# A hybrid encoder layer on eight cores: first two tiles as a pair, earlier first norms, gate rows summed on VectorE, two buffers of normalized chunks, 4 KB weight rows

## The chip, the cores and the metric

The kernel runs on all 8 cores of one Trainium2 chip. The cores share nothing; each works on 6144 of the 49152 positions. Times are device microseconds (us) of the slowest core. The chip's engines appear as PE (TensorE, matmul; PEld its weight loads), DVE (VectorE), ACT (ScalarE), POOL (GpSimd) and SP (SyncE, which here only issues DMAs). Each engine takes its instructions in the order in which the program gives them; a semaphore wait in front of an instruction holds everything behind it on that engine.

## The reference

One layer over 16 prompt sequences of 2048 positions and 4 sample sequences of 4096, each position 1024 wide:

```python
mod = jax.nn.silu(c) @ w_ada + b_ada                    # per sequence, 3 x 1024
shift, scale, gate = jnp.split(mod, 3, axis=-1)
h = rmsnorm(x, norm_g) * (1.0 + scale) + shift
z = h @ w_in                                            # 1024 -> 4608
a, ga, u, v, gb, ma, mb = jnp.split(z, IN_SPLITS, axis=-1)
y_a = fourier_branch(a, w_fmix, b_fmix) * jax.nn.silu(ga)      # 2-D DFT over positions and group channels
y_b = sgu_branch(u, v, ...) * jax.nn.silu(gb)                  # layernorm of v, mixing inside 128 positions
merged = sigmoid(ma) * (y_a @ w_pa) + sigmoid(mb) * (y_b @ w_pb)
out = rmsnorm(x + gate * (merged @ w_out), final_g)
```

The Fourier branch needs all positions of a sequence, so `a` must be known for a whole sequence before any position can be finished. Everything else works on rows of positions.

## The kernel before

A core holds three **units** of 2048 positions, which are three prompt sequences, or one prompt sequence and one sample sequence of two units. The work goes by **tiles** of 512 positions, each of four **chunks** of 128; twelve tiles T, unit u = T // 4. The order of instructions is the order in which the Python code calls helpers. `Sched` keeps one list for each engine and puts semaphore waits before an instruction from what its operands' last writers and readers were; nothing is reordered.

**Front.** Eight 1 MB pieces of `w_ada` come on ACT's queue (`wada_off`), 32 float32 matmuls (L381) give shift and scale for three sequences, 16 small transposes (L389) turn them, and two DVE instructions make the tables `modT` and `Gtab`.

**A block** (`ABlock`): for a whole sequence only the section A of the input projection. A chunk x is loaded on SP's queue into a ring of buffers `XS`, squared and summed on ACT (`x_sq`, L442), 1/root is taken, and the chunk is scaled on DVE (`scale`, L448) to bfloat16 in `xsr`. Four chunks are a group, which `fe2` transposes on PE (32 transposes, L466) and evicts with `Gtab` and `modT`, half on DVE (L474), half on ACT (L479). `a_proj` then has for each chunk eight matmuls (L498), a cast to SBUF on DVE (L312), one first-stage matmul of the DFT (L508), an eviction on ACT or DVE and a store to `Gd` in HBM. In `body`, one pass (a **body**) goes over one group: transposes of the next group, and for each of four chunks the square of a chunk of the group after that, the projection, the first-stage matmul of the chunk before, and one scaling. The root is ACT's `Sqrt` and DVE's reciprocal here (`mode="sqrt"`), and an add and a power on POOL (`rstd`, L433 and L435) elsewhere. Block A does unit 0 (4 groups), block A2 does units 1 and 2 together (8 groups) after tile 3.

**Weights.** `w_in` lies in nine sections of 1 MB in bfloat16 (2 MB float32 in HBM, cast by POOL's DMA): A, V, GB, GA, U, MA0, MB0, MA1, MB1. Each row of a partition is 16 KB in HBM. Section 0 is asked for when piece 6 of `w_ada` is in; sections 1, 2, 3 from the `hooks1` after bodies 0, 1, 2 when a certain projection is done (`("aq", 1, m)`); sections 4 to 8, `w_pa` and `w_pb` from the hook after body 3.

**A tile** goes `v_section`, `silu_section` for GB and GA, U with a product on DVE, `sgu` (PE L686, DVE L692, POOL L697), `fourier_out` (L709 to L712), then eight times `merge_gates` and `merge` (PE L737, L743; DVE L740, L746; POOL L748), then `out_chunk` for four chunks (L610, 16 matmuls each, DVE adds x at L615), of which two are put into the next tile's sections, and `finish` (L624, store to `yu`). The Fourier data are read back from `Gd` (`g2_load`) and combined (`s3s`, L568; `s3j`, L543) between the sections of tiles 0 and 4: in tile 0 one after V, one after GB, two after GA. The normalized chunks of the next tile are made during the merges.

**Gate.** `gate_rows` (L820) multiplies the third part of `w_ada` (eight 512 KB loads) with the three conditions, 16 float32 matmuls of three columns in tile 0, and stores three rows to `gate_d`. In the first tile of each unit (`t == 0`), `w_out` is loaded anew and multiplied by the gate row on POOL (`gate_mul`, L647, eight of 128x1024), two of them in each of the last four merge steps; `out_chunk` reads the whole of `w_out`.

## Time and profile before

| | before |
|---|---|
| median of 3 runs | 1417.32 us (1414.07 to 1423.83) |
| profiled execution | 1415.01 us |
| its span, slowest core | 1413.5 us |
| spans of the cores | 1406.5 to 1413.5 us |
| granted clock of PE, mean | 0.953 to 0.959 |
| PE busy | 1245.9 us (88%) |
| DVE, ACT, POOL busy | 585.4, 503.5, 321.7 us (41, 36, 23%) |
| DMA | 149.84 MB, mean 106 GB/s |

The span runs from a core's first to its last instruction; the time of an execution is 1.5 us longer. All cores have the same program with other data, and their spans lie within 7 us, so that one core stands for all. Busy time of PE is not PE at its peak: a matmul of 512 columns takes 0.216 us from start to start at the full clock, 2.4 GHz, and 0.43 at the lower one, 1.2 GHz.

### The profile page before, as it was taken

What the parts mean: (1) busy time and instruction counts of PE and PEld (TensorE: products, weight loads), DVE (VectorE), ACT (ScalarE), POOL (GpSimd) and SP (SyncE); (2) the same over time, 40 slices, a digit from 0 to 9 for tenths busy, and PEclk for the clock granted to TensorE, in tenths of its full rate; (3) what the DMA queues carried; (4) which work ended last, traced back from release to release, by engine and by line L of the source; (5) the groups of instructions that cost most, each with busy time, mean ns of one, the idle gap of its engine ahead of it and who ended that gap; (6) DMA issues with size and microseconds to landing.
All of it is one profiled execution on the core that took longest, in us unless ns stands there. A gap on an engine that the chain in (4) does not pass through costs nothing.

```text
span 1413.5 us, 19855 instructions; the slowest of 8 cores (1406.5 to 1413.5 us)
## 1 busy us (share of the span) xinstructions
PE 1245.9 (88%) x6412; PEld 601.3 (43%) x6524; DVE 585.4 (41%) x956; ACT 503.5 (36%) x875; POOL 321.7 (23%) x398
## 2 busy tenths in 40 slices
PE   6476299699999997777996999999999699999997
PEld 1243144344444444443543444444444344444443
DVE  0353123344344445665433433444334334444344
ACT  0562213143332436664431334323343233333321
POOL 0000014413032130000145131321313613223122
PEclk9698699899999999999998999999999899999999
DMA  9899952122121255653521221212215112212111
GB/s 285 227 198 170 216 129 90 45 90 90 45 76 60 90 177 172 200 164 109 159 66 45 90 90 45 76 60 90 90 61 135 60 46 75 89 61 91 45 75 60
DMA packets 48503, 149.84 MB, mean 106 GB/s; under 512 B 5772, under 2 KB 18444, under 8 KB 45074
## 3 DMA queue, kind: packets, MB, share of 16 engines
q1 hardware_dynamic: 44514, 122.20, 25.4%
q0 software_dynamic: 2592, 17.96, 7.9%
q10 hardware_dynamic: 1296, 8.40, 1.9%
q8 instruction: 55, 0.90, 0.3%
q14 instruction: 46, 0.38, 0.1%
HBM read 135.03 MB, written 31.47 MB: 118 GB/s over the span
## 4 chain that ended last, share of the span: by engine, by line
PE 76%; DMA 8%; DVE 4%; issue 4%; ACT 4%; POOL 2%; SPq 1%; ACTq 0%; DVEq 0%; POOLq 0%
PE ps L652 41%; PE ps L610 12%; PE ps L743 6%; PE ps L737 6%; DMA Gd<-arena 5%; PE ps L662 5%; PE ps L498 2%; DMA arena<-w_ada 2%; ACT arena L442 2%; POOL arena L647 2%; PE ps L466 2%; ACT arena L479 1%; PE ps L820 1%; DMA arena<-Gd 1%; DVE arena L448 1%
## 5 line engine op out<-in xcount | busy, mean ns | idle before, releaser
L652 PE MATMUL ps<-arena 128*128 128x512 bf16 x2634 | 596.2, 380 | 7.1 <-DVE arena L692 3.7
L652 PEld LDWEIGHTS ps<-arena 128*128 128x128 bf16 x2688 | 262.4, 98 | 319.7 <-issue 8.0
L610 PE MATMUL ps<-arena 128*128 128x512 bf16 x734 | 173.9, 389 | 42.8 <-POOL arena L647 32.0
L729 ACT ACTIVATE arena<-ps 128x512 bf16<-128x512 f32 x192 | 113.2, 597 | 263.2 <-PE ps L652 259.7
L748 POOL TENSOR_TENSOR arena<-arena 128x512 bf16<-128x512 bf16 x96 | 125.1, 1303 | 283.3 <-DVE arena L746 283.3
L740 DVE TENSOR_TENSOR arena<-ps,arena 128x512 bf16<-128x512 f32 x96 | 66.4, 692 | 254.5 <-PE ps L737 254.5
L615 DVE TENSOR_TENSOR arena<-ps,arena 128x512 f32<-128x512 f32 x96 | 66.0, 691 | 189.7 <-PE ps L610 189.7
L610 PEld LDWEIGHTS ps<-arena 128*128 128x128 bf16 x768 | 75.9, 100 | 133.9 <-issue 50.1
L618 ACT ACTIVATE arena<-arena 128x1024 bf16<-128x1024 f32 x48 | 50.7, 1057 | 179.0 <-DVE arena L615 179.0
L442 ACT ACTIVATE arena<-arena 128x1024 bf16<-128x1024 f32 x96 | 100.5, 1047 | 6.1 <-DMA arena<-xB 5.9
L737 PE MATMUL ps<-arena 128*128 128x512 bf16 x384 | 98.6, 379 | 0.0
L743 PE MATMUL ps<-arena 128*128 128x512 bf16 x384 | 98.5, 379 | 0.0
L312 DVE CAST arena<-ps 128x512 bf16<-128x512 f32 (+1 forms) x114 | 64.6, 606 | 81.8 <-DMA Gd<-arena 29.3
L433 POOL TENSOR_TENSOR stat<-stat,eps_sb 128x1 f32<-128x1 f32 x92 | 17.5, 190 | 353.7 <-ACT arena L618 331.2
L498 PE MATMUL ps<-arena 128*128 128x512 bf16 x373 | 90.8, 388 | 5.1 <-DVE arena L312 3.9
L466 PE MATMUL ps<-arena 128*128 128x128 bf16 x768 | 57.9, 245 | 41.8 <-DVE arena L448 41.7
L479 ACT ACTIVATE arena<-ps,modT,Gtab 128x512 bf16<-128x512 bf16 x96 | 67.6, 775 | 75.8 <-PE ps L466 75.8
L662 PE MATMUL ps<-arena 128*128 128x512 bf16 x372 | 85.3, 383 | 0.6
L448 DVE TENSOR_SCALAR arena<-arena,stat 128x1024 bf16<-128x1024 f32 x96 | 73.4, 777 | 6.3 <-ACT arena L729 5.1
L466 PEld LDWEIGHTS ps<-arena 128*128 128x128 bf16 x768 | 54.8, 112 | 48.5 <-issue 45.5
L697 POOL TENSOR_TENSOR arena<-arena 128x512 bf16<-128x512 bf16 x48 | 53.9, 1152 | 92.9 <-DVE arena L692 92.9
L746 DVE TENSOR_TENSOR arena<-ps,arena 128x512 bf16<-128x512 f32 x96 | 66.4, 692 | 16.5 <-PE ps L743 10.3
(79 smaller groups left out, 948.7 us busy)
## 6 DMA issues: line engine op xcount, KB each, us to landing
arena<-xB SPq DMA_DIRECT2D x96, 512.0 KB, 4.0
arena<-xA SPq DMA_DIRECT2D x48, 512.0 KB, 5.1
yu<-arena SPq DMA_DIRECT2D x48, 512.0 KB, 2.8
arena<-w_in POOLq DMA_DIRECT2D x9, 1024.0 KB, 19.4
arena<-w_ada ACTq DMA_DIRECT2D x8, 1024.0 KB, 19.7
Gd<-arena SPq DMA_DIRECT2D x48, 128.0 KB, 2.6
arena<-Gd SPq DMA_DIRECT2D x12, 512.0 KB, 6.9
arena<-w_out POOLq DMA_DIRECT2D x6, 1024.0 KB, 12.8
```

Source lines behind the costliest of these rows:

```text
L442: S.op("act", lambda e: e.activation(out=xsr[:, j, :], in_=fv(XS[k], 1024), func=AF.Square, scale=0.03125, accum_out=stat[:, si, 0:1]), re ...
L448: S.op("dve", lambda e: e.tensor_scalar(out=xsr[:, j, :], in0=fv(XS[k], 1024), scalar1=stat[:, si, 1:2], scalar2=None, op0=ALU.mult), read ...
L466: fns.append(lambda e, b=b, kp=kp, kk=kk, j=j: e.transpose(psb(b)[:, kk * 512 + j * 128: kk * 512 + (j + 1) * 128], xsr[:, j, (2 * kp + kk ...
L479: S.op("act", lambda e, b=b, kk=kk, kc=kc: e.activation(out=hT[:, kc, :], in_=psb(b)[:, kk * 512:(kk + 1) * 512], func=AF.Identity, scale= ...
L498: S.pe([lambda e, kc=kc: e.matmul(ps[b][:], lhsT=hT[:, kc, j * 128:(j + 1) * 128], rhs=w_in_sb[:, 0, kc, :], start=(kc == 0), stop=(kc == ...
L610: S.pe([lambda e, b=b, dmc=dmc, half=half: e.matmul(ps[b][:], lhsT=mg[:, dmc, j * 128:(j + 1) * 128], rhs=w_out_sb[:, dmc, half * 512:(hal ...
L652: S.pe([lambda e, kc=kc: e.matmul(ps[b][:], lhsT=w_in_sb[:, sec, kc, col:col + 128], rhs=hT0[:, kc, :], start=(kc == 0), stop=(kc == 7)) f ...
L662: S.pe([lambda e, kc=kc, b=b, j=j: e.matmul(ps[b][:], lhsT=hT0[:, kc, j * 128:(j + 1) * 128], rhs=w_in_sb[:, SEC["V"], kc, :], start=(kc = ...
L729: S.op("act", lambda e, b=b, so=so: e.activation(out=bv(so, 512), in_=ps[b][:], func=AF.Sigmoid), reads=[("ps", b)], writes=gk(so, 1024))
L737: S.pe([lambda e, k=k: e.matmul(ps[b][:], lhsT=w_pa_sb[:, k, dmc * 128:(dmc + 1) * 128], rhs=sga[:, k, :], start=(k == 0), stop=(k == 3)) ...
L743: S.pe([lambda e, k=k: e.matmul(ps[b2][:], lhsT=w_pb_sb[:, k, dmc * 128:(dmc + 1) * 128], rhs=sgb[:, k, :], start=(k == 0), stop=(k == 3)) ...
L748: S.op("pool", lambda e: e.tensor_tensor(out=mg[:, dmc, :], in0=mg[:, dmc, :], in1=bv(sl[1], 512), op=ALU.add), reads=mk + gk(sl[1], 1024) ...
```

## The change

- **First norms under the load.** The squares and scalings of groups 0 and 1 stand ahead of the adaLN matmuls; chunks 0 to 3 are loaded at once, 4 to 7 when piece 7 of `w_ada` is in. `fe2` is split in `fe_t` (transposes) and `fe_e` (evictions); group 0's transposes stand ahead of the adaLN evictions.
- **Two buffers of normalized chunks.** Groups alternate between `O_XSR` and a second place. Squares are written to a scrap buffer. `sq` now does a pair of chunks: two squares, one `rstd` of width 2 on POOL, always by add and power, and two scalings; it stands ahead of the projections of chunks 0 and 2 of a body. The ring of A2 has 6 chunks instead of 8. Block A takes a sixth group, tile 1's.
- **Tiles 0 and 1 as a pair**, with a second set of buffers (`TB1`, in the place of Z of the other units): V for both, GB for both, and so on; the Fourier pieces stand after GB of tile 0, GB of tile 1, GA of tile 0, GA of tile 1. Output chunks of tile 0 stand after the pair, those of tile 1 in the sections of tile 2.
- **Gate.** Each unit's row is summed on VectorE: eight loads of 128x1024, eight multiply-adds with a condition column (`gate_acc`), then a sum over partitions by two float32 matmuls with a matrix of ones (`gate_sum`). Unit 0 in the merges of tile 0 through two buffers, unit 1 in the merges of tile 2 through one, unit 2 in the sections of tile 3 through three. `gate_mul` is spread: one in each of merge steps 1 to 6, two in step 7.
- **4 KB rows.** The weights lie in HBM as blocks of 1024 columns, so that one row of a transfer is 4 KB; `w_in`, `w_pa`, `w_pb` and `w_out` are loaded so.
- In tile 4 `w_out` is asked for after U instead of before it, and the last two Fourier pieces stand there.

```diff
+    def blocks(t, k):
+        return dram_ap(t, k * 512 * 1024, [[1024, 128], [128 * 1024, 4], [1, 1024]])
+
     def w_sec(s, after=()):
-        S.dma("pool", [lambda e: e.dma_start(
-            out=bv(O_WIN + 8192 * s, 4096), in_=w_in.ap()[s * 128:(s + 1) * 128, :])],
-            "s_w%d" % s, reads=after, writes=wink[s])
+        S.dma("pool", [lambda e: e.dma_start(out=bv(O_WIN + 8192 * s, 4096).rearrange("p (k n) -> p k n", k=4),
+                                             in_=blocks(w_in, s))], "s_w%d" % s, reads=after, writes=wink[s])
...
-    def rstd(n, src, dst, rk, wk, mode):
-
-        if mode == "sqrt":
-            S.op("act", lambda e: e.activation(out=dst, in_=src, func=AF.Sqrt, scale=1.0, bias=eps_sb[:, 0:1]),
-                 reads=rk + ["eps"], writes=wk)
-            S.op("dve", lambda e: e.reciprocal(out=dst, in_=dst), reads=wk, writes=wk)
-        else:
-            S.op("pool", lambda e: e.tensor_tensor(out=dst, in0=src, in1=eps_sb[:, 0:1].to_broadcast([128, n]), op=ALU.add),
-                 reads=rk + ["eps"], writes=wk)
-            S.op("pool", lambda e: e.tensor_tensor(out=dst, in0=dst, in1=mh_sb[:, 0:n], op=ALU.pow),
-                 reads=wk + ["mh"], writes=wk)
...
+    def rstd(n, src, dst, rk, wk):
+
+        S.op("pool", lambda e: e.tensor_tensor(out=dst, in0=src, in1=eps_sb[:, 0:1].to_broadcast([128, n]), op=ALU.add),
+             reads=rk + ["eps"], writes=wk)
+        S.op("pool", lambda e: e.tensor_tensor(out=dst, in0=dst, in1=mh_sb[:, 0:n], op=ALU.pow),
+             reads=wk + ["mh"], writes=wk)
...
+    def sq_op(k, si, junk, jk):
+        S.op("act", lambda e: e.activation(out=junk, in_=fv(XS[k], 1024), func=AF.Square, scale=0.03125,
+                                           accum_out=stat[:, 0, si:si + 1]),
+             reads=gk(XS[k], 4096), writes=jk + [("st", si)])
+
+    def scale_op(k, j, si, xoff):
+        xr = bv(xoff + 2048 * j, 1024)
+        S.op("dve", lambda e: e.tensor_scalar(out=xr, in0=fv(XS[k], 1024), scalar1=stat[:, 1, si:si + 1],
+                                            scalar2=None, op0=ALU.mult),
+             reads=gk(XS[k], 4096) + [("st1", si)], writes=gk(xoff + 2048 * j, 2048))
...
+    def gate_load(kc, k):
+        S.dma("sp", [lambda e: e.dma_start(out=fv(XS[k], 1024), in_=w_ada.ap()[kc * 128:(kc + 1) * 128, 2048:3072])],
+              "s_x%d" % k, writes=gk(XS[k], 4096))
+
+    def gate_acc(u, kc, k, acc):
+
+        c = cs_sb[:, kc * 3 + u:kc * 3 + u + 1]
+        if kc == 0:
+            S.op("dve", lambda e: e.tensor_scalar(out=fv(XS[acc], 1024), in0=fv(XS[k], 1024), scalar1=c, scalar2=None,
+                                                  op0=ALU.mult),
+                 reads=gk(XS[k], 4096) + ["cs"], writes=gk(XS[acc], 4096))
+        else:
+            S.op("dve", lambda e: e.scalar_tensor_tensor(out=fv(XS[acc], 1024), in0=fv(XS[k], 1024), scalar=c,
+                                                         in1=fv(XS[acc], 1024), op0=ALU.mult, op1=ALU.add),
+                 reads=gk(XS[k], 4096) + gk(XS[acc], 4096) + ["cs"], writes=gk(XS[acc], 4096))
...
+            S.pe([lambda e, b=b, h=h: e.matmul(ps[b][:], lhsT=ones_sb[:], rhs=fv(XS[acc], 1024)[:, h * 512:(h + 1) * 512],
+                                               start=True, stop=True)],
...
+        def sq(self, g, h):
+            self.load_to(4 * g + 2 * h + 2)
+            si = stat2(2)
+            for j in (2 * h, 2 * h + 1):
+                sq_op(self.slot(g, j), si + j % 2, bv(O_TYB, 1024), gk(O_TYB, 2048))
+            rstd(2, stat[:, 0, si:si + 2], stat[:, 1, si:si + 2], [("st", si), ("st", si + 1)],
+                 [("st1", si), ("st1", si + 1)])
+            for j in (2 * h, 2 * h + 1):
+                scale_op(self.slot(g, j), j, si + j % 2, self.xoffs[g % 2])
+                self.load_to(4 * g + j + 1 + len(self.ring))
...
         def body(self, hooks):
             for q in range(self.nq):
                 self.fe(q + 1)
                 for j in range(4):
-                    if q + 2 <= self.nq:
-                        self.sq(q + 2, j)
-                    st1 = a_proj(q, j, self.f, 4 * q + j, self.N1)
+                    if q + 2 < len(self.dst) and j % 2 == 0:
+                        self.sq(q + 2, j // 2)
+                    st1 = a_proj(self.dst[q][0], j, self.f, 4 * q + j, self.N1)
                     if self.pend:
                         self.pend.pop(0)()
                     self.pend.append(st1)
-                    self.scales(2)
-                self.scales()
                 if q in hooks:
...
-        gb = [newbank(), newbank()]
-        for kc in range(8):
-            S.pe([lambda e, kc=kc, h=h: e.matmul(ps[gb[h]][0:3, :], lhsT=cs_sb[:, kc * 3:kc * 3 + 3],
-                                                 rhs=fv(XS[kc], 1024)[:, h * 512:(h + 1) * 512],
-                                                 start=(kc == 0), stop=(kc == 7)) for h in range(2)],
...
+    A = ABlock(1, 4, list(range(8)), 16,
+               lambda i: rowsA(i) if i < 16 else rowsB((i - 16) // 4, i % 4),
+               [(hoffs[0], 0), (hoffs[1], 0), (hoffs[0], 0), (hoffs[1], 0), (O_HT, 0), (TB1.h, 0)],
+               (O_XSR, O_Z + 16896))
+    A.load_to(4)
+    S.dma("sp", tabs[1:], "s_tab", writes=["tabs"])
+    tabs = []
+    A.load_to(8, after=gk(wada_off[7], 512))
     A.group(0)
-    A.fe(0)
     A.group(1)
...
+    fe0 = fe_t(A.xoffs[0])
+    for cb in range(4):
+        evict(mrow[0:3, cb * 512:(cb + 1) * 512], ps[mb[cb]][0:3, :], [("ps", mb[cb])], gk(O_MROW + 2048 * cb, 2048))
...
+    fe_e(fe0, hoffs[0], 0)
...
+    pair = (T0, TB1)
+    s3_begin(1)
+    A.fe(5)
+    for tb in pair:
+        v_section(tb)
+    for i, tb in enumerate(pair):
+        silu_section(tb, SEC["GB"], tb.sgb, tb.b)
+        s3s(i)
+    for i, tb in enumerate(pair):
+        silu_section(tb, SEC["GA"], tb.sga, tb.a)
+        s3s(2 + i)
+    w_out_load()
+    gate_load(0, 0)
+    gate_load(1, 1)
+    for tb in pair:
+        u_section(tb)
+    for i, tb in enumerate(pair):
+        sgu(tb)
+        fourier_out(tb, 0, i)
+    merge_gates(T0, 0)
+    for dmc in range(8):
+        if dmc + 1 < 8:
+            merge_gates(T0, dmc + 1)
+        else:
+            merge_gates(TB1, 0)
+        merge(T0, dmc)
+        if dmc % 2 == 0:
+            for k in range(2):
+                gate_acc(0, dmc + k, k, 2)
+                if dmc + k + 2 < 8:
+                    gate_load(dmc + k + 2, k)
+    gate_bias(128, 3)
+    x_load(0, rowsB(2, 0))
+    x_load(1, rowsB(2, 1))
+    sc = []
+    for dmc in range(8):
+        if dmc + 1 < 8:
+            merge_gates(TB1, dmc + 1)
+        merge(TB1, dmc)
+        if dmc == 0:
+            gate_sum(128, 2, 3)
+        else:
+            for k in ((dmc - 1,) if dmc < 7 else (6, 7)):
+                gate_mul(XS[3], k)
+        if dmc in (1, 2, 4, 5):
...
-            if t == 0 and dmc >= 4:
-                gate_mul(u, 2 * (dmc - 4))
-                gate_mul(u, 2 * (dmc - 4) + 1)
+                merge_gates(tb, dmc + 1)
+            merge(tb, dmc)
+            if t == 0 and dmc:
+                for k in ((dmc - 1,) if dmc < 7 else (6, 7)):
+                    gate_mul(O_WIN, k)
+            if T == 2:
+                if dmc:
+                    gate_acc(1, dmc - 1, 6, 7)
+                gate_load(dmc, 6)
...
             A2.fe(0)
             A2.sq(1, 0)
+            out_chunk(tb, T, 0, OS[0])
             A2.sq(1, 1)
-            out_chunk(T, 0, OS[0])
-            A2.scales()
-            A2.sq(1, 2)
-            A2.sq(1, 3)
-            out_chunk(T, 1, OS[1])
-            A2.scales()
-            A2.body({0: lambda: (finish(), out_chunk(T, 2, OS[2])), 1: lambda: (finish(), out_chunk(T, 3, OS[3])),
+            out_chunk(tb, T, 1, OS[1])
```

On DVE, in one body of block A2: before, a reciprocal or one scaling (L448) at a time stands between the casts (L312, of the projections and of every other first stage), and the first two waits of a body are for ACT's root.

```order
L474 TENSOR_SCALAR arena<-ps6,Gtab,modT 128x512
L431 RECIPROCAL stat<-stat 128x1 [waits act]
L312 CAST arena<-ps0 128x512 [waits pe]
L312 CAST arena<-ps1 128x512 [waits pe,s_gw3]
L431 RECIPROCAL stat<-stat 128x1 [waits act]
L312 CAST arena<-ps2 128x512 [waits pe]
L448 TENSOR_SCALAR arena<-arena,stat 128x1024 [waits s_x8,dve]
L431 RECIPROCAL stat<-stat 128x1 [waits act]
L312 CAST arena<-ps4 128x512 [waits pe]
L312 CAST arena<-ps5 128x512 [waits pe,s_gw1]
```

The same place after: evictions are L460, scalings L427, casts L313.

```order
L460 TENSOR_SCALAR arena<-ps6,Gtab,modT 128x512
L427 TENSOR_SCALAR arena<-arena,stat 128x1024 [waits s_x4,pool]
L427 TENSOR_SCALAR arena<-arena,stat 128x1024 [waits s_x5]
L313 CAST arena<-ps0 128x512 [waits pe,dve]
L313 CAST arena<-ps1 128x512 [waits pe,dve,s_gw3]
L313 CAST arena<-ps2 128x512 [waits pe,dve]
L427 TENSOR_SCALAR arena<-arena,stat 128x1024 [waits s_x6,pool]
L427 TENSOR_SCALAR arena<-arena,stat 128x1024 [waits s_x7]
L313 CAST arena<-ps4 128x512 [waits pe,dve]
```

Two scalings with a wait for POOL now stand ahead of the cast of chunk 0, and two more ahead of that of chunk 2.

On PE, from the last transposes of the A block of unit 0 on: before (L662 is V, L652 the other sections, L568 and L576 the Fourier pieces).

```order
L662 MATMUL ps<-arena 128x512 x32
L568 MATMUL ps<-arena 128x128 x16
L576 MATMUL ps<-arena 128x64 x4
L652 MATMUL ps<-arena 128x512 x32
L568 MATMUL ps<-arena 128x128 x16
```

After (V is L687, the other sections L677, Fourier pieces L557 and L565, transposes L447):

```order
L447 MATMUL ps<-arena 128x128 x32
L687 MATMUL ps<-arena 128x512 x64
L677 MATMUL ps<-arena 128x512 x32
L557 MATMUL ps<-arena 128x128 x16
L565 MATMUL ps<-arena 128x64 x4
L677 MATMUL ps<-arena 128x512 x32
L557 MATMUL ps<-arena 128x128 x16
```

96 section matmuls stand ahead of the first Fourier piece where 32 stood, and 32 transposes of tile 1 ahead of them.

On POOL, the weight loads behind block A: before, sections 1 to 6 follow one another with nothing between.

```order
L837 DMA arena<-w_sT 128x512
L369 DMA arena<-w_in 128x4096 [waits pe]
L369 DMA arena<-w_in 128x4096 [waits pe,s_w0]
L369 DMA arena<-w_in 128x4096 [waits pe,s_wa5]
L369 DMA arena<-w_in 128x4096 [waits s_wa4]
L369 DMA arena<-w_in 128x4096 [waits s_wa7]
```

After, from section 2 on:

```order
L373 DMA arena<-w_in 128x4x1024 [waits pe,s_w0]
L408 TENSOR_TENSOR stat<-stat,eps_sb 128x2 [waits act,dve]
L410 TENSOR_TENSOR stat<-stat,mh_sb 128x2 [waits pool]
L408 TENSOR_TENSOR stat<-stat,eps_sb 128x2 [waits act,dve]
L410 TENSOR_TENSOR stat<-stat,mh_sb 128x2 [waits pool]
L373 DMA arena<-w_in 128x4x1024 [waits pe,s_wa5]
```

The same four instructions stand once more between section 3 and section 4: every section now goes out behind the norms (L408, L410) of a body, which wait for ACT's squares; before, section 4 stood right behind section 3.

## Rows read from the trace of the kernel before

**Rows 1.** The page, busy tenths of PE in 40 slices of the span.
```profile
PE   6476299699999997777996999999999699999997
```

**Rows 2.** Waits of PE, whole span: waiting line, releaser; total, times, longest, us.
```profile
PE ps L466 <- DVE arena L448: 41.7, 10, 9.8
PE ps L610 <- POOL arena L647: 32.0, 3, 10.7
PE ps L568 <- DMA arena<-Gd: 25.2, 1, 25.2
```

**Rows 3.** DMA of the first 40 us: packets, MB and rate.
```profile
DMA packets 2733, 11.71 MB, mean 293 GB/s; under 512 B 937, under 2 KB 937, under 8 KB 1693
```

**Rows 4.** Timeline of the opening, PE: start, length, engine, line, what, [idle before].
```profile
39.45 3.59 PE L381 MATMUL ps<-arena,cs_sb 128*3 128x512 f32 x8 [1.22 <-DMA arena<-w_ada]
44.08 1.12 PE L389 MATMUL ps<-id_sb,arena 3*128 3x3 f32 x16 [1.04 <-ACT arena L442]
...
65.09 3.15 PE L466 MATMUL ps<-arena 128*128 128x128 bf16 x28 [9.78 <-DVE arena L448]
```

**Rows 5.** Timeline of PE from 120 to 206 us.
```profile
132.72 8.22 PE L662 MATMUL ps<-arena 128*128 128x512 bf16 x31
166.13 1.86 PE L568 MATMUL ps<-arena 128*128 128x128 bf16 x16 [25.20 <-DMA arena<-Gd]
...
192.08 13.89 PE L820 MATMUL ps<-arena,cs_sb 128*3 128x512 f32 x32
```

**Rows 6.** Chain of waits around the Fourier data of unit 0: start, length, what.
```profile
145.93 14.53 DMA Gd<-arena
160.63 5.26 DMA arena<-Gd
```

**Rows 7.** Timeline of three bodies of the second A block.
```profile
606.54 3.33 PE L466 MATMUL ps<-arena 128*128 128x128 bf16 x32 [2.57 <-DVE arena L448]
...
611.31 1.05 ACT L442 ACTIVATE arena<-arena 128x1024 bf16<-128x1024 f32 x1
...
620.82 1.95 PE L466 MATMUL ps<-arena 128*128 128x128 bf16 x32 [2.57 <-DVE arena L448]
...
624.64 1.06 ACT L442 ACTIVATE arena<-arena 128x1024 bf16<-128x1024 f32 x1
...
626.38 1.29 DVE L312 CAST arena<-ps 128x512 bf16<-128x512 f32 x2
...
627.33 0.38 PE L508 MATMUL ps<-arena 128*128 128x512 bf16 x1 [0.89 <-ACT arena L442]
...
632.61 1.41 DVE L448 TENSOR_SCALAR arena<-arena,stat 128x1024 bf16<-128x1024 f32 x2
...
634.16 1.95 PE L466 MATMUL ps<-arena 128*128 128x128 bf16 x32 [2.57 <-DVE arena L448]
```

**Rows 8.** Timeline of GpSimd: add and power of width 1, then power of width 4.
```profile
538.96 0.19 POOL L433 TENSOR_TENSOR stat<-stat,eps_sb 128x1 f32<-128x1 f32 x1 [8.69 <-ACT arena L618]
...
539.29 0.55 POOL L435 TENSOR_TENSOR stat<-stat,mh_sb 128x1 f32<-128x1 f32 x1
...
280.82 1.02 POOL L435 TENSOR_TENSOR bnag<-bnag,mh_sb 128x4 f32<-128x4 f32 x1
```

**Rows 9.** Timeline at the end of the merges of the first gated tile.
```profile
258.00 4.22 POOL L647 TENSOR_TENSOR arena<-arena 128x1024 bf16<-128x1024 bf16 x2
...
262.86 1.49 PE L610 MATMUL ps<-arena 128*128 128x512 bf16 x3 [10.67 <-POOL arena L647]
```

**Rows 10.** Timeline of two more operations, then DMA issues: count, size, median us to landing.
```profile
208.69 4.49 POOL L697 TENSOR_TENSOR arena<-arena 128x512 bf16<-128x512 bf16 x4 [21.58 <-DVE arena L692]
...
282.06 2.48 DVE L624 SCALAR_TENSOR_TENSOR arena<-arena,stat 128x1024 f32<-128x1024 f32 x2
...
arena<-xB SPq DMA_DIRECT2D x96, 512.0 KB, 4.0
...
arena<-w_ada SPq DMA_DIRECT2D x8, 512.0 KB, 12.9
```

445 lines of the change are left out of this document (233 added, 212 removed).

## The prediction

> **What bounds the kernel now.** I read the page first: the profiled execution took 1415.0 us, its slowest core's span is 1413.5 us, so 1.5 us lie around the span, and the median of the runs is 1417.3 us. PE is busy in nine tenths of most slices; the low ones stand in the first fifth of the span and around slices 15 to 19 [rows 1]. That is where time can be won: some 1246 us of PE work stay whatever the order. Next the waits of PE over the whole span [rows 2]: transposes waiting for normalized chunks (VectorE L448) 41.7 us in 10 waits, output projections waiting for gate multiplies (GpSimd L647) 32.0 us in 3, and one 25.2 us wait for the Fourier data of unit 0. Then the timeline of the opening and the chain of waits, to see which wait ends last there.
>
> The opening goes so. The adaLN weights come in at 293 GB/s with the DMA engines full [rows 3], the last adaLN matmul starts at 39.4 us, and only then are x chunks normalized; the transposes of group 1, which I call T(1), start at 65.1 [rows 4]. Four bodies of four chunks follow; tile 0's V section starts at 132.7 at a low clock (8.2 us; at the full one 31 such matmuls take 6.9), then PE waits until 166.1 [rows 5], because the last store of the Fourier data was on its way for 14.5 us after it was issued [rows 6]: 16 KB rows of weights filled the DMA engines. At 192.1 PE spends 13.9 us on float32 gate matmuls with three columns [rows 5].
>
> **The change part by part,** as differences in us of the span.
>
> *Front end.* The bytes that must land before the second group is transposed are the same: w_ada 8.4 MB, eight chunks 4.2, section 0 2.1, 14.7 MB in all; at [rows 3]'s rate they end near 48 us. The order changes: chunks 4 to 7 are asked for only when the last adaLN piece is in. ScalarE's adaLN evictions stand behind the square of chunk 7, VectorE's behind its scaling. So: 47.5, square 1.1 [rows 7], GpSimd pair 1.2, two scalings 1.4, two row copies 1.4 (the last two took 1.04 ahead of the small transposes [rows 4]), sixteen small transposes 1.1, and T(1) starts near 54, 11 us earlier.
>
> *Bodies of the A blocks (two buffers, chunks normalized in pairs).* This is the term that decides. A body is T, four projections, four first-stage matmuls. I take the old one from [rows 7]: T at 620.8, then ScalarE's four evictions and at 624.6 the square (T + 3.8), root and reciprocal, the cast at 626.4, the first-stage matmul at 627.3 (T + 6.5); the scalings hold the next T until 634.2. T to T is 14.3 and 13.3, mean 13.8. Now VectorE's row has two scalings ahead of the cast that the first-stage matmul needs, and they wait for two squares and for GpSimd. T + 3.8 squares start; second square ends at + 6.2 (1.25 and 1.15); GpSimd add and power of width 2: 0.14, 0.33 and a power between 0.55 (width 1) and 1.02 (width 4) [rows 8], 0.7, so + 7.4; two scalings + 8.9; cast 0.7 and 0.25: first-stage matmul at T + 9.8. PE has finished T and two projections at + 5.2, so it waits 4.6 us. The same again for the second pair: 0.5 to ScalarE's eviction, 0.5 until its square starts, 2.4, 1.2, 1.5, 0.7, 0.25, that is 7.1; the matmul 0.2. Next T at T + 17.0. The wait of T for scalings goes, as meant, and a longer one takes its place in the middle of the body. At the low clock the squares start 1.0 later (611.3 is T + 4.8, against 3.8) [rows 7], so 18.0; I take 17.4, the clock being low in part. Bounds: 13.3 (the pair order costs nothing) and 18.7 (low clock in both halves).
>
> The first block: four bodies at 17.4, 2.3 for ScalarE's eight extra evictions in the first, 3.5 for the channel tables, 2 for the transposes of tile 1: V starts at 54 + 77.4 = 131.4 instead of 132.7: **-1.3**. The second block: seven bodies with squares, 3.6 each, and 2 more at its entry, where the pair stands ahead of the output additions: **+27**.
>
> *The pair.* Before the first Fourier blocks are needed there is now V, V and GB, 20.7 us, where there was V. The last store is issued near 132. The seven late weight loads now stand on GpSimd's queue behind the norms of the last body, near 129 instead of 99 to 115, so the stores meet a less filled DMA, and 4 KB rows let them between. Block 0 landed 5.3 us after its load was asked for [rows 6]; even 12 us would be in time for 153. So the 25.2 go, **-25.2**, and 1 of low clock, **-1**. The late weights (seven of 2.1 MB at [rows 3]'s rate, 50 us) are in by 180; the first used of them, U, is due at 188: hidden. It costs 15 us if they start 20 late. Two sgu stages in a row run into GpSimd's product of 1.12 us a head [rows 10] with a ring of two: PE waits for banks, **+3.6** (0 to 6). Everything else of the two tiles is the same PE work.
>
> *Gates.* Matmuls of 13.9 go, two float32 matmuls with a matrix of ones come, 0.86 each (L381's four, in eight records, took 3.6) [rows 4]: **-12.1**. Units 1 and 2 had their gates from the same pass, so they pay the two matmuls again: **+3.4**. The 24 multiply-adds of 1.24 us (two of that form took 2.48) [rows 10] lie on VectorE beside 5.2 us of PE per step, under the matmuls. In tile 2 they go through one buffer: load, add, load. With 4.0 us to land, as xB chunks do, and 1.3 for the add with its wait, a turn is 5.5 against 5.2: **+2** (bounds 0, and the rival below).
>
> *Gate multiplies spread over the merges.* At the end of a gated tile GpSimd had two merge additions and four multiplies left; now one addition and two multiplies. Four multiplies take 8.4 us (4.2 for two), of which half goes, and PE's 10.7 us wait [rows 9] becomes 6.7: three times **-4.0**, -12 (bounds -6 and -24).
>
> Sum: -1.3 + 27 - 25.2 - 1 + 3.6 - 12.1 + 3.4 + 2 - 12 = -15.6, a span of 1398. With 1.5 around it 1399.4; the median before was 2.3 above the profiled execution, and I say **1401 us**, 1.2% less. Over 1% is about what a measurement of this kernel can tell from no change.
>
> **The rivals.** *A: the pair order costs nothing in the bodies.* For it: most of the 41.7 us [rows 2] are what a second buffer is there to remove. Against: VectorE takes its instructions in order. With 13.3 per body the second block gives -3.5 instead of +27, and V starts 16 earlier in the first: 1401 - 46 = 1355, or 1372 where late weights and Fourier loads then bind the pair. *B: the clock falls in every body.* After the same 2.57 us wait T took 3.33 us once and 1.95 twice [rows 7], at 1.2 and 2.4 GHz; with waits of 4.6 and 3.3 us in each body both halves may start low: 18.7 instead of 17.4, eleven times, +14: 1415. The Trainium skill (TensorE: Matmul & The Clock Gate, HAM oscillation) describes a kernel whose every step begins at half clock because a wait stands in each; by that rule B is what happens, and the trace agrees in one body of three. *C: the gate's single buffer paces tile 2* (slower). The SyncE queue puts each gate load behind the multiply-add of the one before, and x loads and stores behind it; VectorE, waiting for a load, holds the merge products, and PE runs out of banks. It decides from 5 us landing. The gate loads of before took 12.9 us in the median [rows 10], though eight at once beside weights: 12.9 + 1.5 - 5.2 is 9.2, eight times 74, 1475; at 8 us 34, 1435. For it: nothing hides a turn. Against: the DMA engines are mostly idle there, and a lone chunk lands in 4.0. *D: the cut rows do not free the stores.* If a store still takes some 27 us and the Fourier blocks come at 178, PE waits 24 at 154 and the pair buys next to nothing: 1425. The Trainium skill (DMA: Bandwidth & Descriptors, SWDGE vs HWDGE vs iDMA) says an engine changes rings only between packets, preferably of at most 4096 bytes; by that the cut rows should shorten each turn fourfold, which speaks against D; no row here has such rows.
>
> **How the numbers follow.** Forecast (1385 to 1410) 0.42, A 0.22, B 0.15, C 0.11, D 0.10. The forecast's own range comes from its bounds: the bodies 16.7 to 17.8, the front end 5 either way, multiplies and sgu. The range for all reaches into A at its bound side and into D, 1364 to 1430; C beyond it and the fast end of A are left out, 2 in 10. Faster by over 1% (under 1403): A and three fifths of the forecast, with a little, 0.52. Within 1%: the rest of the forecast, B: 0.30. Slower: C, most of D's upper side and B's: 0.18.
>
> **What would show it.** T to T in the second block near 17, with waits of PE L497 (first stage) for VectorE of 4 to 5 us twice a body, and the waits of the transposes for the scalings gone; V of tile 0 near 131; no wait of L557 for the Fourier load above 2 us; L610 waiting for GpSimd 6 to 7 us three times; tile 2's merges at 5.2 us a step. What would make it wrong: bodies of 14 us (A), transposes of 3.4 us in all of them (B), merge steps over 6 us in tile 2 (C), PE idle at GB or U of the pair (D).

## The result: 1% slower

The changed kernel took 1433.2 us in the median of four runs (1431.2 to 1434.9), the kernel before 1420.6 beside it: ratio 1.0104, 95% interval 1.0056 to 1.0151. I had said 1401, with a range up to 1430, and a gain. The profiled execution has a span of 1432.2 us against 1413.5, so 18.7 us are to be found. By the medians they are 12.6: the traced execution of the kernel before, 1415.0 us, was 5.6 us below the median of its runs here, so that a span compared with its span looks some 6 us worse than the medians do. Ratios and medians here and below are over the runs in which no die was slowed.

The page of the changed kernel, PE and its clock in 40 slices, then two rows of DMA issues (count, size, median us to landing):

```profile
PE   6566799989989896677898999999999899999997
PEclk9798899999999998888999999999999999999999
...
arena<-w_ada SPq DMA_DIRECT2D x24, 512.0 KB, 4.8
...
Gd<-arena SPq DMA_DIRECT2D x48, 128.0 KB, 3.5
```

The low slices stand where they stood [rows 1], in the first fifth and, counted from 0, at 15 to 18. The waits of PE over the whole span show what changed (waiting line, releaser; us in total, times, longest):

```profile
PE ps L497 <- DVE arena L313: 65.9, 25, 5.1
PE ps L604 <- POOL arena L672: 18.9, 3, 6.3
PE ps L879 <- DVE arena L313: 14.1, 1, 14.1
...
PE ps L651 <- DVE arena L639: 10.1, 2, 5.2
PE ps L557 <- DMA arena<-Gd: 7.5, 2, 7.1
PE ps L447 <- DVE arena L427: 7.1, 1, 7.1
```

The 41.7 us of transposes waiting for scalings [rows 2] are 7.1 now. In their place the first stage (L497) waits 65.9 us for casts, the small transposes (L879) 14.1, and the ones matmuls (L651) 10.1, a wait that I had not named. The 32.0 us for gate multiplies are 18.9, the 25.2 for the Fourier data 7.5.

One body of the second A block, timeline of PE and of VectorE (start, length, engine, line, what, [idle before]); it answers to [rows 7]:

```profile
605.50 1.95 PE L447 MATMUL ps<-arena 128*128 128x128 bf16 x32
607.29 1.89 PE L487 MATMUL ps<-arena 128*128 128x512 bf16 x8
609.01 0.38 PE L497 MATMUL ps<-arena 128*128 128x512 bf16 x1
609.23 1.89 PE L487 MATMUL ps<-arena 128*128 128x512 bf16 x8
615.27 0.58 PE L497 MATMUL ps<-arena 128*128 128x512 bf16 x1 [4.15 <-DVE arena L313]
615.65 3.62 PE L487 MATMUL ps<-arena 128*128 128x512 bf16 x8
619.06 0.63 PE L497 MATMUL ps<-arena 128*128 128x512 bf16 x1
619.49 2.40 PE L487 MATMUL ps<-arena 128*128 128x512 bf16 x8
622.44 0.38 PE L497 MATMUL ps<-arena 128*128 128x512 bf16 x1 [0.55 <-DVE arena L313]
```

```profile
613.00 1.42 DVE L427 TENSOR_SCALAR arena<-arena,stat 128x1024 bf16<-128x1024 f32 x2 [3.77 <-POOL stat L410]
614.33 1.88 DVE L313 CAST arena<-ps 128x512 bf16<-128x512 f32 x3
620.16 1.42 DVE L427 TENSOR_SCALAR arena<-arena,stat 128x1024 bf16<-128x1024 f32 x2 [3.96 <-POOL stat L410]
```

VectorE idles 3.77 us ahead of two scalings whose rstd is not there, while casts that could run stand behind them; PE gets its first-stage input 9.8 us after T, at 615.27. Behind its wait the third projection takes 3.62 us, 1.2 GHz, and the next part of the fourth is still slow. T to T is 17.2 (605.50, 622.65), as forecast. At the end of the body PE waits only 0.55 us, where I had said 3.3: the projections at the low clock fill that time, and the period is set by ScalarE, GpSimd and VectorE.

Where the 18.7 us come from, segment by segment, against the terms of the prediction (differences of the changed kernel's span from the kernel before; the starts are those of [rows 4, 5 and 7] and of the timelines here):

| stretch | said | measured |
|---|---|---|
| T(1) of the first block | -11.1 | -2.7 (62.4) |
| from there to V of tile 0 | +9.8 | +16.5 (V at 146.5) |
| V of tile 0 to the first merges, both tiles | -36.5 | -29.1 |
| ones matmul of unit 0 | +1.7 | +2.2 |
| gate multiplies of tile 0 | -4 | -5.4 |
| tile 1's own transposes, which went ahead of V | 0 | -2.6 |
| gates of units 1 and 2, in tiles 2 and 3 | +5.4 | +20.8 |
| second A block | +27 | +25.7 |
| the rest, with two sets of gate multiplies | -8 | -6.6 |
| sum | -15.7 | +18.8 |

Up to rounding the columns add up to the prediction's -15.6 and to the 18.7. The transposes of tile 1 are a slip of my sum: their 2 us were charged to the first block and not taken off where they had stood. Each stretch is from one traced execution of either kernel. Three stretches carry the miss: the opening with the first block, the Fourier data, and above all the gates of tiles 2 and 3.

### The profile page after: what moved, and what is told of

It is laid out like the page before. It is cut to its first block, busy times and chain, and to the rows that moved or that the text cites. A ratio compares the mean times of both kernels' runs of the same rounds, so it can differ in the third digit from the quotient of the medians.

```text
span 1432.2 us, 20068 instructions; the slowest of 8 cores (1425.6 to 1432.2 us)
## 1 busy us (share of the span) xinstructions
PE 1269.4 (89%) x6504; PEld 602.3 (42%) x6504; DVE 610.8 (43%) x933; ACT 485.2 (34%) x818; POOL 352.7 (25%) x442
## 4 chain that ended last, share of the span: by engine, by line
PE 70%; DMA 11%; DVE 5%; ACT 5%; issue 5%; POOL 3%; SPq 0%; ACTq 0%; DVEq 0%; POOLq 0%
PE ps L677 38%; PE ps L604 11%; PE ps L773 5%; PE ps L767 5%; PE ps L687 4%; DMA arena<-w_ada 4%; DMA arena<-Gd 3%; ACT arena L421 3%; DMA Gd<-arena 2%; ACT arena L465 2%; DVE arena L313 1%; PE ps L487 1%; POOL stat L410 1%; DMA arena<-xA 1%; POOL arena L672 1%
## 5 line engine op out<-in xcount | busy, mean ns | idle before, releaser
L677 PE MATMUL ps<-arena 128*128 128x512 bf16 x2688 | 602.6, 380 | 1.7 <-DVE arena L724 1.6
L677 PEld LDWEIGHTS ps<-arena 128*128 128x128 bf16 x2688 | 262.7, 98 | 319.6 <-issue 8.4
L604 PE MATMUL ps<-arena 128*128 128x512 bf16 x768 | 178.8, 391 | 28.8 <-POOL arena L672 18.9
L408 POOL TENSOR_TENSOR stat<-stat,eps_sb 128x1 f32<-128x1 f32 (+1 forms) x114 | 25.3, 222 | 509.4 <-ACT arena L612 317.5
L427 DVE TENSOR_SCALAR arena<-arena,stat 128x1024 bf16<-128x1024 f32 x96 | 71.5, 771 | 166.5 <-POOL stat L410 166.4
L604 PEld LDWEIGHTS ps<-arena 128*128 128x128 bf16 x768 | 76.2, 100 | 125.0 <-issue 41.9
L612 ACT ACTIVATE arena<-arena 128x1024 bf16<-128x1024 f32 x48 | 50.7, 1057 | 186.5 <-DVE arena L609 186.5
L487 PE MATMUL ps<-arena 128*128 128x512 bf16 x384 | 112.2, 446 | 0.3 <-ACT arena L465 0.3
L773 PE MATMUL ps<-arena 128*128 128x512 bf16 x384 | 98.6, 379 | 0.0
L767 PE MATMUL ps<-arena 128*128 128x512 bf16 x384 | 98.5, 379 | 0.0
L313 DVE CAST arena<-ps 128x512 bf16<-128x512 f32 (+1 forms) x114 | 62.7, 602 | 62.3 <-PE ps L557 21.2
L687 PE MATMUL ps<-arena 128*128 128x512 bf16 x384 | 84.7, 379 | 0.0
L497 PE MATMUL ps<-arena 128*128 128x512 bf16 x48 | 22.1, 460 | 65.9 <-DVE arena L313 65.9
L776 DVE TENSOR_TENSOR arena<-ps,arena 128x512 bf16<-128x512 f32 x96 | 66.3, 691 | 16.7 <-PE ps L773 11.2
L410 POOL TENSOR_TENSOR stat<-stat,mh_sb 128x1 f32<-128x1 f32 (+1 forms) x114 | 67.7, 594 | 17.3 <-POOL stat L408 1.5
```

The costliest lines, as they stand in the source:

```text
L313: S.op("dve", lambda e: e.tensor_copy(out=dst, in_=src), reads=reads, writes=writes)
L410: S.op("pool", lambda e: e.tensor_tensor(out=dst, in0=dst, in1=mh_sb[:, 0:n], op=ALU.pow), reads=wk + ["mh"], writes=wk)
L487: S.pe([lambda e, kc=kc: e.matmul(ps[b][:], lhsT=hT[:, kc, j * 128:(j + 1) * 128], rhs=w_in_sb[:, 0, kc, :], start=(kc == 0), stop=(kc == ...
L604: S.pe([lambda e, b=b, dmc=dmc, half=half: e.matmul(ps[b][:], lhsT=tb.mg[:, dmc, j * 128:(j + 1) * 128], rhs=w_out_sb[:, dmc, half * 512:( ...
L677: S.pe([lambda e, kc=kc: e.matmul(ps[b][:], lhsT=w_in_sb[:, sec, kc, col:col + 128], rhs=tb.hT[:, kc, :], start=(kc == 0), stop=(kc == 7)) ...
L687: S.pe([lambda e, kc=kc, b=b, j=j: e.matmul(ps[b][:], lhsT=tb.hT[:, kc, j * 128:(j + 1) * 128], rhs=w_in_sb[:, SEC["V"], kc, :], start=(kc ...
```

## The experiments

Each was timed beside the kernel before; the ratio is to the runs of the same batch. The span is that of the profiled execution, and times at single stages are from that one execution.

| kernel | median us | ratio to before, 95% interval | span us |
|---|---|---|---|
| changed | 1433.2 | 1.0104 (1.0056 to 1.0151) | 1432.2 |
| e1_lag | 1387.4 | 0.9769 (0.9723 to 0.9814) | 1385.7 |
| e2_front | 1431.5 | 1.0063 (1.0037 to 1.0089) | 1429.8 |
| e3_gates | 1424.2 | 1.0014 (0.9991 to 1.0038) | 1425.3 |
| e4_rows16 | 1457.2 | 1.0243 (1.0208 to 1.0277) | 1455.5 |
| e5_pipe | 1374.9 | 0.9652 (0.9636 to 0.9669) | 1373.7 |
| e6_before_rows4 | 1410.2 | 0.9904 (0.9886 to 0.9923) | 1410.1 |
| e8_best | 1359.9 | 0.9549 (0.9534 to 0.9565) | 1356.7 |
| e9_order | 1340.4 | 0.9450 (0.9431 to 0.9469) | 1338.2 |
| e10_mul | 1337.4 | 0.9431 (0.9407 to 0.9456) | 1335.5 |
| e11_onebuf | 1357.4 | 0.9569 (0.9545 to 0.9593) | 1353.2 |
| e12_all | 1316.0 | 0.9246 (0.9222 to 0.9271) | 1312.2 |
| e13_after_order | 1430.3 | 1.0058 (1.0039 to 1.0076) | 1426.9 |

### The order on VectorE

**e1_lag.** The scalings of a pair stand behind the second cast after them.

```diff
                 for j in range(4):
                     if q + 2 < len(self.dst) and j % 2 == 0:
-                        self.sq(q + 2, j // 2)
+                        sc.append(self.sq(q + 2, j // 2, lag=True))
...
                     self.pend.append(st1)
+                    if sc and j % 2:
+                        sc.pop(0)()
```

> The changed kernel, but in both A blocks the two scalings of a pair stand on VectorE's queue behind the cast of the second projection after them, not ahead of the cast of the first. Theory (VectorE's order is the cost of the pairs: it stands 5.73 and 3.91 us a body in front of a scaling whose rstd is not there, with ready casts behind it): the waits of the first stage (L497) for the cast, 4.2 and 1.7 us, go; the last scaling of a body now ends about 11.5 us after its transposes began, so that the period of the second block falls from 17.2 to about 12, 8 times 5 = 41 us less, and about 3 times 4 less in the first block: near 1385 to 1395 us. Rival (the bodies are bound by something else that would show up at once, the six-chunk ring and its loads, or the chain square, square, rstd, scale, scale of two pairs, 3.8 + 3.8 us and the evictions ahead of them): the period stays at 16 or more and the time within 5 us of 1433.

The theory held, and the order turned out to be the whole term: with it changed the second block is faster than in the kernel before (115.1). From T(1) to the V of tile 4 the second block took 108.6 us instead of 140.7, from T(1) to the V of tile 0 the first took 74.2 instead of 84.1; the span is 46.5 less. I had said a period of 12, 41 and 12 us less; it was 32.1 and 10.0. One period, PE:

```profile
575.41 3.57 PE L447 MATMUL ps<-arena 128*128 128x128 bf16 x32 [2.03 <-DVE arena L427]
578.78 2.88 PE L487 MATMUL ps<-arena 128*128 128x512 bf16 x8
...
587.32 0.38 PE L497 MATMUL ps<-arena 128*128 128x512 bf16 x1
589.82 2.52 PE L447 MATMUL ps<-arena 128*128 128x128 bf16 x32 [2.12 <-DVE arena L427]
```

The period of 14.4 here and 13.5 behind it, where I had said 12, is the wait for the last scaling and the clock behind it: transposes of 3.57 and a projection of 2.88 where the full clock gives 1.95 and 1.89. The next kernel takes both away.

**e5_pipe.** Squares and rstd stand one pair ahead of the scalings.

```diff
                     if q + 2 < len(self.dst) and j % 2 == 0:
-                        self.sq(q + 2, j // 2)
+                        self.scales(q + 2, j // 2)
+                        g, h = (q + 2, 1) if j == 0 else (q + 3, 0)
+                        if g < len(self.dst):
+                            self.squares(g, h)
```

> The changed kernel, but the squares and rstd of a pair stand one pair ahead of its scalings, so that each scaling finds its rstd ready. In the kernel with the scalings behind the second cast the period of the second block was 13.5 us, of which 2.1 to 2.8 are a wait of the transposes for the last scaling, and another 2 are transposes and first projection at the low clock behind that wait. Theory (the order on VectorE was the whole cost of the pair; ScalarE, VectorE and TensorE each have 9 to 10 us of work a body): the period falls to 10 to 11, the second block from its second transposes to the V of tile 4 from 140.7 us to 85 to 90; the first block gains at most as much as with the lag, since stores of Gd wait there for the DMA; 1370 to 1380 us. Rival (the six-chunk ring or the eight stores and loads on SyncE's queue take over at once): the period stays at 13 or more, near 1390.

The period is 10.0:

```profile
575.87 1.95 PE L447 MATMUL ps<-arena 128*128 128x128 bf16 x32
...
585.66 0.38 PE L497 MATMUL ps<-arena 128*128 128x512 bf16 x1
585.87 1.95 PE L447 MATMUL ps<-arena 128*128 128x128 bf16 x32
```

PE goes from transposes to transposes at 2.4 GHz; the rival, a ring of six chunks or SyncE's queue, did not show. The second block took 93.9 us, 47 less than in the changed kernel; I had said 85 to 90, and the first three bodies, which also hold output projections, are the difference (T to T 17.0, 14.6 and 11.1). The first block took 69.7, 4.5 less than in e1_lag, where I had said that it gains no more than there; PE stood 17.6 us of it before one first-stage matmul, as it did in e8_best below.

**e11_onebuf.** One buffer of normalized chunks instead of two, in e8_best.

```diff
-               (O_XSR, O_Z + 16896))
+               (O_XSR, O_XSR))
...
-                        [(hoffs[g % 2], 1 + g // 4) for g in range(8)] + [(O_HT, 1)], (O_XSR, XS[10]),
+                        [(hoffs[g % 2], 1 + g // 4) for g in range(8)] + [(O_HT, 1)], (O_XSR, O_XSR),
```

> The combined version with one buffer of normalized chunks in both A blocks instead of two. Theory (the second buffer is worth little: what cost the kernel before 41.7 us of waits of transposes for scalings was that squares, rstd and scalings of a chunk stood in the same body; with the squares a pair ahead a scaling can run as soon as the transposes of that body have read the buffer): the period of the second block stays at 10 to 11 and the time within 4 us of 1361. Rival (the second buffer is what the second block lives on, and the order only lets it work): the period rises to 12 or more, 15 us or more in all.

The second block took 94.2 us against 93.8 with two buffers, the ratios agree within their intervals. Under this order the second buffer bought nothing; under the order of the changed kernel, or of the kernel before, it was not tested. Rival A of the prediction was right that a body of 13 us and less was to be had, and wrong that the buffer would give it.

### Rows of 4 KB, and what stands ahead of a store

**e4_rows16.** The changed kernel with weights in rows of 16 KB.

```diff
-        S.dma("pool", [lambda e: e.dma_start(out=bv(O_WIN + 8192 * s, 4096).rearrange("p (k n) -> p k n", k=4),
-                                             in_=blocks(w_in, s))], "s_w%d" % s, reads=after, writes=wink[s])
+        S.dma("pool", [lambda e: e.dma_start(out=bv(O_WIN + 8192 * s, 4096), in_=w_in.ap()[s * 128:(s + 1) * 128, :])],
+              "s_w%d" % s, reads=after, writes=wink[s])
```

> The changed kernel with the weights again in rows of 16 KB instead of 4 KB. Theory (rows decide how long a store of 128 KB stands behind the weights, but the first block is held by VectorE's order and by the total of bytes): stores in the first block take longer than in the changed kernel, the wait for the first Fourier load grows from 7.1 us to 10 or more, the time is 0 to 8 us more, up to 1441. Rival (4 KB rows cost more descriptors on GpSimd's queue and slow the weights down): 3 to 8 us less.

The direction was right, the size, 23.3 us of span, three times what I had allowed. In the first block the rows changed nothing, against what I had said: V starts at 145.1 against 146.5. The waits of PE, first of this kernel, then of the changed kernel's timeline at the same place, with its issue of the four Fourier loads and, from its chain of waits, the last store and the fourth of the loads:

```profile
PE ps L557 <- DMA arena<-Gd: 30.1, 1, 30.1
```

```profile
160.35 7.07 PE L677 MATMUL ps<-arena 128*128 128x512 bf16 x32
174.56 1.86 PE L557 MATMUL ps<-arena 128*128 128x128 bf16 x16 [7.13 <-DMA arena<-Gd]
...
157.39 11.03 SPq L520 DMA_DIRECT2D arena<-Gd  x4
...
146.28 10.94 DMA Gd<-arena
159.35 41.73 DMA arena<-Gd
```

With rows of 16 KB the last store takes 25.8 us instead of 10.9, the Fourier loads are asked for at 170.8 instead of 157.4, and the first block of them is used at 196.1 instead of 174.6. With all of the change but the rows the stall is longer than it was before (25.2), not shorter: with either rows the last seven weight loads are issued near 140 to 146 us, at the last stores, and in the kernel before at 99 to 115. There they were in when the first Fourier load was asked for, and it took 5.3 us [rows 6]. In the changed kernel they land until 208: the first Fourier load takes 16.7 us, the fourth 41.7, and PE waits 7.1 us for the first and reaches the others at most 2 us after they land.

**e6_before_rows4.** The same rows in the kernel before, nothing else.

```diff
-        S.dma("pool", [lambda e: e.dma_start(
-            out=bv(O_WIN + 8192 * s, 4096), in_=w_in.ap()[s * 128:(s + 1) * 128, :])],
+        S.dma("pool", [lambda e: e.dma_start(
+            out=bv(O_WIN + 8192 * s, 4096).rearrange("p (k n) -> p k n", k=4), in_=blocks(w_in, s))],
```

> The kernel before, with the weights in rows of 4 KB and nothing else. With 16 KB rows the changed kernel waited 30.1 us for its first Fourier load instead of 7.1, and took 23 us more. Theory (the rows, not the pair, took most of the 25.2 us stall away): the stall before the first Fourier blocks falls from 25.2 to 5 to 10 us and the time by 15 to 20, near 1402 to 1408. Rival (it is the pair's cover, V and V and GB instead of V alone, and rows only matter on top of it): the stall stays over 18 and the time within 7 us of the kernel before.

Neither story as I wrote it. The waits of PE for the Fourier data, total, times, longest:

```profile
PE ps L571 <- DMA arena<-Gd: 23.7, 2, 21.1
```

The rows brought the first Fourier block from 166.1 to 155.9, half of it as an earlier V (127.7 against 132.7), and 1.0% of the time by the ratio, 14 us; the spans of the two traced executions differ by 3.4 alone. But the stall stays at 21: the block comes 28.2 us after V starts, in the changed kernel 28.0, in e5_pipe 28.5. The pair covers that with its own work and leaves 7. The last stores take 8.6 to 10 us here instead of 14.5 to 27, but the load behind them takes 15.0 instead of 5.3, with the weights still under way. So the rows and the pair each did a part of what I had booked for the pair. The pair without the rows, in the kernel before, was not run; e4_rows16 suggests that it would have bought nothing at this place.

**e9_order.** e8_best (below) with V's and GB's weights after the third body, the final norm's table after the block.

```diff
-        tab(fg_bc, dram_ap(final_g, 0, [[0, 128], [1, D]]))
...
-        0: lambda: (late_tabs(), w_s_load(), w_sec(1, after=[("aq", 1, 0)])),
-        1: lambda: w_sec(2, after=[("aq", 1, 4)]),
-        2: lambda: (channel_tables(), w_sec(3, after=[("aq", 1, 8)])),
+        0: lambda: (late_tabs(), w_s_load()),
+        2: lambda: (channel_tables(), w_sec(1), w_sec(2), w_sec(3)),
```

> The combined version, with the weights of V and GB loaded after the third body of the first block instead of after the first and second, and the final norm's table after the block instead of after its first body. In the combined version TensorE stands 19.6 us in the third body, since a cast waits for the place of a store of Gd that was issued near 82 us behind 3 MB of tables and weights and landed near 105. Theory (the order of the bytes is that wait, their sum sets the first Fourier load, 34 to 35 MB by 154 us in the combined version): the wait falls under 8 us, V starts at 113 to 118 instead of 127.2, but V and GB may wait for their own weights, and the first Fourier block starts within 4 us of 153.9; time within 4 us of 1361. Rival (the stores' lateness is what delays the Fourier loads): the first Fourier block starts before 148 and 6 to 10 us go.

The reason for trying it, in e8_best: the chain of waits in the first block, and PE behind it.

```profile
79.22 27.09 DMA Gd<-arena
...
107.02 0.69 DVE arena L313
...
107.96 0.58 PE ps L497
```

One store of 128 KB took 27.1 us, and the cast that needs its place waited; the bodies, at 10 us each, had caught up with the DMA. My theory fell, the rival held: the longest wait for a cast went from 19.6 to 4.3 us, V started at 111.0 instead of 127.2, and the first Fourier block at 137.4 instead of 153.9, 16.5 earlier with the same weights to come. The span fell by 18.5 us, where the rival had said 6 to 10. PE of e9_order there:

```profile
111.00 13.98 PE L686 MATMUL ps<-arena 128*128 128x512 bf16 x64
124.81 7.07 PE L676 MATMUL ps<-arena 128*128 128x512 bf16 x32
137.35 1.86 PE L556 MATMUL ps<-arena 128*128 128x128 bf16 x16 [5.48 <-DMA arena<-Gd]
```

Nothing waited for V's or GB's weights. It was not the sum of the bytes that held this block back, but which of them stood ahead of the stores.

**e13_after_order.** The same edit in the changed kernel alone.

```diff
-        0: lambda: (late_tabs(), w_s_load(), w_sec(1, after=[("aq", 1, 0)])),
-        1: lambda: w_sec(2, after=[("aq", 1, 4)]),
-        2: lambda: (channel_tables(), w_sec(3, after=[("aq", 1, 8)])),
+        0: lambda: (late_tabs(), w_s_load()),
+        2: lambda: (channel_tables(), w_sec(1), w_sec(2), w_sec(3)),
```

> The changed kernel with only the later loads of V's and GB's weights and of the final norm's table. In the changed kernel the third body of the first block waits 4.2, 3.6 and 3.4 us for casts, two of them for the place of a store of Gd that is still under way. Theory (the order of the bytes is worth what VectorE's own order leaves of it): the bodies of the first block all take 17 to 18 us, V of tile 0 starts near 139 instead of 146.5, the first Fourier block near 167 instead of 174.6: 7 us less, near 1426. Rival (as in the combined version, the stores' lateness costs the whole block): 15 to 20 us less, near 1416.

V of tile 0 at 139.0, the first Fourier block at 166.7: these two as the theory said. The span is 5.3 less, for 7. In the changed kernel a store of 21.6 us stood in its third body (the chain of waits):

```profile
94.60 21.57 DMA Gd<-arena
```

ScalarE's eviction waited 11.1 us for its place, and the squares, the rstd, the scalings and the casts stood behind; the store before it, of 21.1 us, held a cast 5.9 us by itself. The third body took 27.4 us there and takes 19.2 here. The intervals of the ratios, 1.0058 and 1.0104, overlap, so that the gain in time is not shown by itself; the reading rests on the stages of one traced execution each.

### The opening

**e2_front.** The norms of chunks 4 to 7 behind the adaLN evictions and the first evictions of transposes.

```diff
     A.group(0)
-    A.group(1)
...
     fe_e(fe0, hoffs[0], 0)
+    A.group(1)
     A.body(hooks1)
```

> The changed kernel, but the norms of chunks 4 to 7 stand behind the adaLN evictions and behind the evictions of the first transposes. Theory (the 14.1 us for which TensorE stands before its 3x3 transposes have two covers: the order on ScalarE and VectorE, and behind it the landing of chunks 4 to 7 at 49 to 55 us, which is the DMA's doing): the 3x3 transposes start near 47 us instead of 60.7, the second transposes still wait for chunk 7 and start near 59.5 instead of 62.4, the first projection near 61.5 instead of 66.3: 5 us less in all, near 1428. Rival (the order alone is the cost): the second transposes start near 50 and 10 to 13 us go, near 1421.

The small transposes started at 46.1, but T(1) at 60.5 instead of 62.4, and the span is 2.4 us less: half of what I had said, and the chunks' landing, not the order, is what holds T(1). ScalarE of the changed kernel in the opening:

```profile
25.01 1.06 ACT L421 ACTIVATE arena<-arena 128x1024 bf16<-128x1024 f32 x1 [3.98 <-DMA arena<-xA]
...
49.98 1.06 ACT L421 ACTIVATE arena<-arena 128x1024 bf16<-128x1024 f32 x1 [23.82 <-DMA arena<-xA]
...
55.47 1.06 ACT L421 ACTIVATE arena<-arena 128x1024 bf16<-128x1024 f32 x1 [0.61 <-DMA arena<-xA]
...
56.53 1.05 ACT L311 ACTIVATE arena<-ps 3x512 f32<-3x512 f32 x2
```

Chunk 4 is there at 50 and chunk 7 at 55.5. I had put chunk 7 at 47.5, from the bytes and the 293 GB/s of the kernel before; the changed kernel moved 262, 275 and 257 GB/s in its first three stretches of 20 us. The trace shows where it fell behind. Chunks 4 to 7 are asked for at 38.5, when the last piece of w_ada has landed, and by then the DMA has run dry: 66 and 83 GB/s from 36 to 38 and 38 to 40 us, where the kernel before, which had asked ahead, moved 348 and 361. Its chunk 7 landed at 50.7. No run asked for the chunks earlier, so what that gives back is not measured.

### The gates of units 1 and 2

**e3_gates.** Two buffers in tile 2, the ones matmuls of tile 3 behind the Fourier output.

```diff
-                    gate_acc(1, dmc - 1, 6, 7)
-                gate_load(dmc, 6)
+                    gate_acc(1, dmc - 1, (6, 12)[(dmc - 1) % 2], 7)
+                if dmc == 0:
+                    gate_load(0, 6)
+                if dmc < 7:
+                    gate_load(dmc + 1, (12, 6)[dmc % 2])
+                else:
+                    gate_bias(1, 6)
```

> The changed kernel, but in tile 2 the gate's weights go through two buffers (the second one is the place of the normalized V, free by then) and its bias is loaded ahead, and in tile 3 the ones matmuls stand behind the Fourier output instead of ahead of the spatial products. Theory (TensorE's 5.19 and 4.91 us before the ones matmuls are VectorE's accumulations, in tile 2 held up by a load into the single buffer, 4.00 and 3.64 us, in tile 3 by the queue of its own work): both waits go, the ones matmuls run at the full clock, 1.9 us each instead of 3.5 and 3.75, and the start of the second A block moves from 527.6 to near 514: 13 to 15 us less, near 1419. Rival (VectorE's 16 passes of 1.28 us are themselves too much for the merges, so that the wait only moves to the next consumer): less than 5 us, near 1430.

What it is about, in the changed kernel: the last merge steps of tile 2 on PE, VectorE at their end, then PE in tiles 2 and 3.

```profile
410.02 1.03 PE L767 MATMUL ps<-arena 128*128 128x512 bf16 x4
415.20 1.03 PE L767 MATMUL ps<-arena 128*128 128x512 bf16 x4
...
420.29 1.28 DVE L639 SCALAR_TENSOR_TENSOR arena<-arena,cs_sb 128x1024 f32<-128x1024 f32 x1 [2.33 <-DMA arena<-w_ada]
...
426.77 1.28 DVE L639 SCALAR_TENSOR_TENSOR arena<-arena,cs_sb 128x1024 f32<-128x1024 f32 x1 [4.00 <-DMA arena<-w_ada]
431.70 1.28 DVE L639 SCALAR_TENSOR_TENSOR arena<-arena,cs_sb 128x1024 f32<-128x1024 f32 x1 [3.64 <-DMA arena<-w_ada]
432.90 1.89 DVE L460 TENSOR_SCALAR arena<-ps,Gtab,modT 128x512 bf16<-128x512 bf16 x4
```

```profile
424.33 3.61 PE L604 MATMUL ps<-arena 128*128 128x512 bf16 x16 [3.72 <-POOL arena L778]
433.13 3.47 PE L651 MATMUL ps<-arena,ones_sb 128*128 128x512 f32 x4 [5.19 <-DVE arena L639]
...
479.50 3.75 PE L651 MATMUL ps<-arena,ones_sb 128*128 128x512 f32 x4 [4.91 <-DVE arena L639]
```

A step of the merges stays at 5.2 (410.02, 415.20), so the single buffer doesn't hold the merges. Its own turns take 4.9 to 6.5 us (420.29, 426.77 is the longest), 5.7 in the mean of seven, of which a load is 3.6 to 5.1 and the multiply-add 1.3; so the accumulation is 3.4 us late after seven turns. The larger part is its place: the seventh multiply-add stands behind the last merge's products, the eighth waits for a load that can be asked for only behind the seventh, and the evictions of the next transposes and the ones matmul stand behind the eighth, which ends at 433.0, 14.3 us after the transposes began. The edit took out 8.7 of the 20.8 us (from the V of tile 2 to the second block 186.4 instead of 195.1), not 13 to 15: the last load was still asked for only at 421.3, and in tile 3 the ones matmul, now behind the sgu, waited 2.75 us for the sgu's operation on VectorE (L724), which the multiply-adds stand ahead of. The median is 9.0 us less than that of the changed kernel; the mechanism stands, my remedy was half of one.

**e8_best.** e5_pipe, e2_front, and the gate weights loaded ahead of the merges, so that the accumulation keeps step with them; the ones matmuls of tile 3 after its first merge.

```diff
             if T == 2:
-                if dmc:
-                    gate_acc(1, dmc - 1, 6, 7)
-                gate_load(dmc, 6)
+                gate_acc(1, dmc, (6, 12)[dmc % 2], 7)
+                if dmc < 6:
+                    gate_load(dmc + 2, (6, 12)[dmc % 2])
+                elif dmc == 6:
+                    gate_bias(1, 6)
+            if T == 3 and dmc == 0:
+                gate_sum(1, 7, 6)
+                gate_store(2, 6)
+                A2.load_to(6)
```

> The changed kernel with squares and rstd one pair ahead, the norms of chunks 4 to 7 behind the adaLN evictions, tile 2's gate weights in two buffers with their first loads ahead of the merges, and tile 3's ones matmuls behind the first merge. If the costs add: the second block as in the kernel with the squares ahead, 50 to 55 us less than in the changed kernel, the front end 2 less, the gates 12 to 15 less (with the ones matmuls placed behind the second tile's Fourier output, 2.7 us and the low clock were left of them): 1355 to 1368 us. Rival (the front end and the first block are bound by the bytes that they load, so that what is saved there comes back as a wait for the Fourier loads): the first Fourier block starts no earlier than 158 us and 5 us less are gained, 1365 to 1375.

1359.9 us. The costs add: against the changed kernel 75.5 us of span, of which the two blocks make up 63 (46.9 and 16.2), the opening 3.2 and the gates 9.2, not the 12 to 15 that I had said: tile 3 still waits 2.75 us for the sgu on VectorE, and the 32 matmuls behind it run partly at the low clock (8.75 us for 7.07). The rival on bytes did not hold: the first Fourier block came at 153.9, where it had said 158 or later, and e9_order takes the rest of its reason away.

### The gate multiplies, and all together

**e10_mul.** e8_best with two multiplies after the third and sixth merges and none after the eighth.

```diff
+    MUL = {1: (0,), 2: (1, 2), 3: (3,), 4: (4,), 5: (5, 6), 6: (7,)}
...
-            for k in ((dmc - 1,) if dmc < 7 else (6, 7)):
+            for k in MUL.get(dmc, ()):
                 gate_mul(XS[3], k)
```

> The combined version, with the last gate multiply ahead of the seventh merge's addition instead of two behind the eighth: two multiplies after the third and the sixth merge, where GpSimd has no rstd. Theory (what is left of the wait before the first output of a gated tile, 6.3 us three times, is one addition and two multiplies of 2.1 us; the multiplies depend on no merge): the three waits fall to 2.2 us, as in tiles without gates, and the outputs behind them run at the full clock: 12 to 15 us less, near 1347. Rival (two multiplies in one step of 5.2 us hold the rstd or the addition behind them, and the wait moves to the scalings): 0 to 5 us less.

21.2 us of span less than e8_best, more than I had said, of which 15.0 can be laid to the multiplies: from the transposes of tile 2 to its V 17.3 us instead of 24.4, and from the V of tile 4 to the end 7.9 less for the other two. The rest lies in other waits of the two executions. Part of the gain is the clock behind the wait. PE before the first outputs, first e8_best, then e10_mul:

```profile
297.99 16.31 PE L604 MATMUL ps<-arena 128*128 128x512 bf16 x64 [6.29 <-POOL arena L672]
```

```profile
290.45 13.97 PE L604 MATMUL ps<-arena 128*128 128x512 bf16 x64 [1.50 <-POOL arena L672]
```

**e12_all.** Both edits, and six of the seven late weight loads held until the Fourier loads are in.

```diff
-        3: lambda: (w_sec(4), w_sec(5), w_sec(6), w_pab(), w_sec(7), w_sec(8)),
+        3: lambda: w_sec(4),
...
         v_section(tb)
+    g2k = gk(O_WOUT, 16384)
+    w_sec(5, after=g2k)
+    w_sec(6)
+    w_pab()
+    w_sec(7)
+    w_sec(8)
```

> The combined version with the later loads of V's and GB's weights and of the final norm's table, with the gate multiplies two steps earlier, and with six of the seven late weight loads held on GpSimd's queue until the four Fourier loads of the first unit have landed. Moving the two weight loads and the table gave 20 us, the multiplies 23. If they add: 1316 to 1322 us before the third edit. In the version with the later loads the first Fourier block waited 5.5 us, and the last store of Gd was issued some 26 us ahead of it. Theory (the Fourier loads share the DMA with 7 MB of weights issued just ahead of them): the wait goes, 5 to 8 us with the low clock behind it, and nothing waits for the later weights: 1308 to 1316. Rival (the held weights are late for U and the merges): a wait of the U section or the first merges of 5 us or more takes its place, 1316 or above.

1316.0 us, 7.5% under the kernel before, at the upper end of what I had said. The wait before the first Fourier block fell to 2.2 us, and no section waited for a weight:

```profile
133.85 1.08 PE L556 MATMUL ps<-arena 128*128 128x128 bf16 x16 [2.17 <-DMA arena<-Gd]
```

The third edit is worth the 3.5 us by which that block comes earlier than in e9_order, with V at the same 111.0: said were 5 to 8. The first load takes 12.2 us for 14.5, and all four are in by 139.9 instead of 161.6. So the weights beside them make the loads slow, but hardly more than these 3.5 us can be had by holding them back.

## Why the prediction was wrong, step by step

**Right, with their sizes.** The bodies, the term that I said decides: 17.2 measured for 17.4, +25.7 for +27, with waits of L497 of 4.2 us in the middle (3.4 to 5.1 in all) and 0.5 to 1.7 at the end. The second wait I had at 3.3; the time went into projections at the low clock instead, so that the period came out by the same chain of square, rstd, scaling and cast. Rival A, that the pair order costs nothing, is refuted: e1_lag and e5_pipe show that the pairs' place on VectorE's queue was all of it, and e11_onebuf that under the better order the second buffer is worth nothing. The gate multiplies, three times -4.0: -5.4 in tile 0 and -6.6 with the rest for the other two; the wait is 6.3, three times, as said. The two sgu stages, +3.6: from 216.0 to 224.5 they took 8.5 us where two sets of 3.1 stood, +2.3. Rival B: the clock fell in every body, and stayed at 1.2 GHz for the third projection and part of the fourth; so much was in the 17.4. The Trainium skill (TensorE: Matmul & The Clock Gate, HAM oscillation) describes steps that each begin at half clock behind a wait. The trace agrees for what follows the 4.2 us wait in the middle of each body; the body's start, behind 0.6 us, is at the full clock.

**"So: 47.5 ... T(1) starts near 54": the landing, 8.4 us off.** The last chunk came at 55.5. Some 2.7 us of the miss are my division: 14.7 MB at 293 GB/s are 50.2 us, not 48 or 47.5, and the kernel before had its own chunk 7 only at 50.7. The rest is the order of the requests, which I had taken as free: with chunks 4 to 7 asked for behind the last piece of w_ada, the DMA moved 66 and 83 GB/s around 38 us instead of 348 and 361. That is read from the traces; no run moved the request. The chain behind it was right to 0.5 us (55.5 to 62.4 is 6.9; said 6.5).

**"The first block: four bodies at 17.4": 6.7 us off.** Not the bodies in general, but stores of Gd of 21.1 and 21.6 us in the third, for whose places a cast and an eviction had to wait. I had taken the stores for free once the rows were cut; with two weight loads and a table moved (e13_after_order) the block took 75.5 us instead of 84.1, 1.9 under the forecast.

**"So the 25.2 go": 7.4 us off, and for another reason than said.** I had the last store issued near 132 and the Fourier block by 153. It was 146 and 174.6. Of the two steps behind V, the store took 10.9 us, and the load 16.7, where I had "5.3 us after its load was asked for" and "even 12 us would be in time": that 5.3 was measured when the late weights were in, and now they were under way beside it until 208, not 180. From V to the block it is 26.4 to 28.5 us in every kernel with 4 KB rows and the late weights at this place but e1_lag (23.6), and 22.8 in e12_all, which holds them back. "Hidden", as U's need of them, they were. What saved the pair was the edit that I gave no price of its own: 4 KB rows, 23 us of span in the changed kernel (e4_rows16) and 3.4 of span, 14 in the median, in the kernel before (e6_before_rows4). Rival D had this as its case, and its price, 24 us, is about what e4_rows16 measured, 23.3 of span on top of the changed kernel. From 140 to 175 us a packet of GpSimd's queue kept its DMA engine for 0.78 us in e4_rows16 (621 packets in 86.5% of the 16 engines' time) and for 0.22 in the changed kernel (1955 in 75.9%). The Trainium skill (DMA: Bandwidth & Descriptors, SWDGE vs HWDGE vs iDMA) has it that an engine turns to another ring only between packets; these packets, and the last store's 25.8 against 10.9 us, agree with it.

**"A turn is 5.5 against 5.2: +2", and "+3.4" for the ones matmuls: 15.4 us off, the largest miss.** Tile 2 costs 12.1 of the 20.8 and tile 3 8.7. The size of the turn was nearly right, 5.7 in the mean for 5.5, and the merges kept their 5.2 us a step, so that rival C, which had the buffer pace them, did not come. What failed is that I costed the term by its throughput. I asked only whether the multiply-adds fit beside PE's work per step, not who stands behind the last one: the evictions of the next transposes in tile 2, the ones matmul itself in both, and then float32 matmuls at the low clock, 3.5 and 3.75 us for 1.9. PE waited 3.7 and 5.2 us in tile 2 and 4.9 in tile 3. e3_gates took 8.7 us of it back and e8_best 9.2; of the 11.6 that are left in e8_best 3.4 are the ones matmuls as booked, 4.4 are the wait for the sgu on VectorE in tile 3, behind two multiply-adds, with its clock, and the rest holds a wait of 2.2 us and the low clock before the outputs of tile 2. No run took these apart. Gates off PE's path were booked as -12.1 +3.4 +2 = -6.7; they were worth -13.9 +2.2 +20.8, that is +9.1.

So the 34 us between -15.6 and +18.7 are 8.4 in the opening, 6.7 in the first block, 7.4 before the Fourier data and 15.4 at the gates, less some 3.5 elsewhere, of which the 2.6 for tile 1's transposes is luck: a slip of the sum. It was no one mechanism but four places where something stands behind an instruction or a transfer and I had costed it at nothing.

## What to carry to other kernels

When an engine takes its instructions in order, ask of each that is put in its row how long it will wait there and what ready work stands behind; a step of lead does away with the wait (e5_pipe: 58.5 us of span), and with that lead a second buffer was worth nothing (e11_onebuf). A small store on whose place a loop waits is on the critical path as soon as the loop is faster than the bytes ahead of the store: order the bytes by when they are needed, not by when their place is free (e9_order: 18.5 us of span). Don't hold requests back until the queue has run dry (the opening; read from the traces, not tested by a run). And cost every moved accumulation by the operation behind its last element, not by its throughput.

## What was not expected of the hardware

The size of the rows of one queue's loads set the time of another queue's stores and loads: cut from 16 to 4 KB, with the same bytes, the first Fourier block landed 21.5 us sooner in the changed kernel and 10.3 in the kernel before, half of it there by an earlier V. A single store of 128 KB, 3.5 us to its landing in the median of the changed kernel, took 27.1 us in e8_best behind tables and weights.

The first outputs after a wait of 2.2 us (e8_best, ahead of tile 3) took 5.30 us for sixteen matmuls against 3.62 at the full clock, while in the changed kernel sixteen such behind a wait of 3.7 took 3.61 and the float32 matmuls behind the next wait 3.47 instead of 1.9. How the clock falls after a wait was not settled by these runs; that a wait removed can give back more than its length was seen in e10_mul: 4.8 us of wait and 2.3 of clock before the first outputs.
